# Rotated query columns of two heads in one stationary operand of 128 columns, rotation in blocks of 64 partitions

## The chip, the cores and the metric

The kernel is one program on one core of a Trainium2 chip. It is measured in microseconds (us) of device time of one launch. All arithmetic that matters is in 32-bit floats; a product of two such matrices is made from three products of operands that are split into a high part and a low part.

## What is computed

The program runs two blocks of a model over 256 tokens of width 1024. Its first mixer is a latent attention of 8 heads, and the change lies in there. Cut to what matters:

```python
def mla_mixer(x, w_dq, q_norm_g, w_uq, w_dkv, kv_norm_g, w_ukv, w_o):
    cq = rms_norm(x @ w_dq, q_norm_g)                          # 256 x 384
    q = (cq @ w_uq).reshape(b, s, H, NOPE + ROPE)              # 8 heads of 128 + 64 columns
    ckv_kr = x @ w_dkv                                         # 256 x (256 + 64)
    ckv = rms_norm(ckv_kr[..., :KV_LORA], kv_norm_g)
    kv = (ckv @ w_ukv).reshape(b, s, H, NOPE + V)
    k_nope, v = kv[..., :NOPE], kv[..., NOPE:]
    q_nope = q[..., :NOPE]
    q_rope = apply_rope(q[..., NOPE:], cos[:, None, :], sin[:, None, :])
    k_rope = apply_rope(ckv_kr[..., KV_LORA:], cos, sin)       # one for all heads
    # per head: softmax((q_nope k_nope^T + q_rope k_rope^T) * scale) @ v
    return o.reshape(b, s, H * V) @ w_o
```

Behind it come a gated feed-forward layer with a short convolution, a differential attention, two more feed-forward layers, a hybrid mixer, and a last feed-forward layer.

## The kernel before, in words

Five instruction streams are written out by hand, one for each engine (`sp`, `pe`, `act`, `dve`, `pool` in the code), and they meet at semaphores. There is no scheduler: the order of each engine is the order in which its code is written, and an engine that waits holds back all that is written behind the wait.

**Units of weights.** The weights come from HBM in units. Units 0 and 1 are `w_dq`, 2 and 3 `w_dkv`, 4 to 7 `w_uq` (`U_UQ`, two heads or 384 columns each, three chunks of 128 rows), 8 and 9 `w_ukv` (`U_UKV`), 10 to 13 `w_o`. A unit passes four stages, with two slots of each buffer, so unit u follows unit u - 2 in its slot:

- SyncE (`load_unit`, L397 to L415) loads it into `raw_u` in two DMAs, for the first and the second half of its chunks (one chunk and two for units 4 to 7). It waits until ScalarE and VectorE have split unit u - 2.
- ScalarE (`split_u`, L1302) rounds it into `hi_u`. It waits for the landing of each half and for the last use of unit u - 2 by TensorE (`used_u`).
- VectorE (`split_half`, L1787) writes the rest into `lo_u`.
- TensorE multiplies. It may start on the first chunk when that half is split, and waits for the other (`rest_ready`, L646) ahead of the second chunk.

**Queries.** For each unit of `w_uq` TensorE (L836 to L862) makes the two heads' 128 plain columns (`features_out`, 9 matmuls a head, the weights stationary, 128 columns of them) and then the two heads' 64 rotated columns (9 matmuls a head, 64 columns of stationary operand, into partitions 0 to 63 of a PSUM bank). ScalarE copies the plain part to `m_q` (L1530). VectorE (L2012 to L2027) rotates the rotated part of both heads at once: a product with the cosines over 64 partitions and 512 elements, two products with the sines over 32 partitions, which write across to the other half, and an addition into `m_qr`. `m_qr` and the rotated key `m_kr` have zeros in partitions 64 to 127. TensorE then waits for VectorE's reads of a bank before it writes that bank again (`m_qr_read`), and before it starts unit 9 it waits for all four rotations (`m_qr_out`, L874).

**Keys.** VectorE rotates the key token by token in `kr3` (L2000 to L2004), TensorE transposes it (L861), ScalarE copies it to `m_kr` (L1528). Then TensorE makes keys and values from units 8 and 9, and the attention over 8 heads follows.

The functions around this are below, with the line numbers of the profile.

## Time and profile before

| | |
|---|---|
| Three runs | 1192.35 us median, 1192.18 to 1193.42 |
| Span of the profiled execution, first to last instruction | 1190.5 us (its time outside the span is not recorded apart) |
| TensorE busy | 1150.6 us, 97% of the span |
| VectorE, ScalarE, GpSimd busy | 809.4, 702.7, 52.4 us |
| Read from HBM | 192.84 MB |
| Mean granted TensorE clock | 0.998 of full speed |

PE is TensorE, PEld its weight loads, DVE VectorE, ACT ScalarE, POOL GpSimd, SP SyncE and SPq its DMA issues. A busy time of PE counts from the start of a matmul to its modelled end, and matmuls overlap, so the cost of one is read from the distance of two starts. Every row has its start in us from the start of the span. Where the text says a "gap", the engine was idle before the row for the time in square brackets. The latent attention's queries, keys and values fill 28.2 to 58.3 us of the span.

### The profile page before, as it was taken

To read this page: it belongs to the slowest core of one execution; us is meant where nothing else is said; L and a number is where in the kernel's file an instruction comes from. 1 tells how busy PE (TensorE), PEld (TensorE's weight loads), DVE (VectorE), ACT (ScalarE), POOL (GpSimd) and SP (SyncE) were. 2 spreads that over 40 slices of the span, in tenths; PEclk is the share of its full clock that TensorE was granted. 3 is DMA by queue.
4 is the path that set the end of the run, shared out by engine and by line. 5 is a ranking of instruction groups with operands and counts; after the bars stand their busy time and mean duration, and the time that the engine had idled before them with its cause. 6 is when DMAs were issued, how large, how long until landed. Compare 5 with 4: busy or idle time off the path is not lost. (4 is left out here: it accounts for less than half of the span.)

```text
span 1190.5 us, 19157 instructions
## 1 busy us (share of the span) xinstructions
PE 1150.6 (97%) x6611; PEld 983.5 (83%) x6611; DVE 809.4 (68%) x1206; ACT 702.7 (59%) x1218; POOL 52.4 (4%) x74
## 2 busy tenths in 40 slices
PE   9999999999999989999999999999989999999997
PEld 7977888888799868888887888888977877888886
DVE  6855888888656568888877665565656756656555
ACT  6455666666566557766666554555565655555543
POOL 0200000000100010000001000000000320000000
PEclk9999999999999999999999999999999999999999
DMA  7515566667244446666673666653674016767661
GB/s 229 184 41 167 158 198 209 187 183 242 86 142 141 145 127 190 200 189 192 195 211 99 201 191 182 207 156 112 196 217 147 1 36 174 211 176 197 186 168 62
DMA packets 241057, 194.56 MB, mean 163 GB/s; under 512 B 11214, under 2 KB 223792, under 8 KB 241008
## 3 DMA queue, kind: packets, MB, share of 16 engines
q1 hardware_dynamic: 240928, 193.88, 54.1%
q8 instruction: 30, 0.49, 0.2%
q14 instruction: 19, 0.16, 0.0%
q10 hardware_dynamic: 80, 0.03, 0.0%
HBM read 192.84 MB, written 1.05 MB: 163 GB/s over the span
## 5 line engine op out<-in xcount | busy, mean ns | idle before, releaser
L767 PE MATMUL psum<-act_hl,hi_u 128*128 128x512 f32 x1312 | 327.6, 392 | 3.1 <-DVE lo_u L1813 3.1
L1813 DVE TENSOR_TENSOR lo_u<-raw_u,hi_u 128x2048 fp32r<-128x2048 f32 x103 | 236.1, 2292 | 88.4 <-ACT hi_u L1319 56.1
L767 PEld LDWEIGHTS psum<-act_hl,hi_u 128*128 128x128 f32 x1312 | 240.9, 188 | 50.5 <-issue 3.7
L770 PEld LDWEIGHTS psum<-act_hl,lo_u 128*128 128x128 f32 x1312 | 179.0, 190 | 12.8
L770 PE MATMUL psum<-act_hl,lo_u 128*128 128x256 f32 x1312 | 182.9, 282 | 0.0
L1439 ACT ACTIVATE arena<-psum 128x256 f32<-128x256 f32 x174 | 66.1, 380 | 157.0 <-PE psum L770 146.7
L1920 DVE TENSOR_TENSOR arena<-psum,arena 128x256 f32<-128x256 f32 x174 | 73.6, 423 | 106.0 <-ACT arena L1439 105.9
L622 PE MATMUL psum<-hi_d,hid_hi 128*128 128x512 f32 (+1 forms) x352 | 138.8, 394 | 1.6 <-DVE hid_lo L1937 1.6
L1337 ACT ACTIVATE hi_u<-raw_u 128x2048 fp32r<-128x2048 f32 x72 | 137.3, 1907 | 4.2 <-DMA raw_u<-in_ffn_w_gu 4.0
L623 PE MATMUL psum<-lo_d,hid_hi 128*128 128x512 f32 (+1 forms) x352 | 137.9, 392 | 0.0
L624 PE MATMUL psum<-hi_d,hid_lo 128*128 128x512 f32 (+1 forms) x352 | 137.0, 389 | 0.0
L1930 DVE SCALAR_TENSOR_TENSOR arena<-arena,vecs 128x255 f32<-128x255 f32 x176 | 85.0, 483 | 42.4 <-ACT arena L1447 31.4
L1818 DVE TENSOR_TENSOR lo_d<-raw_d,hi_d 128x1024 fp32r<-128x1024 f32 x88 | 106.6, 1216 | 3.1 <-ACT hi_d L1346 3.1
L1796 DVE TENSOR_TENSOR lo_u<-raw_u,hi_u 128x1024 fp32r<-128x1024 f32 (+4 forms) x74 | 79.4, 1108 | 43.1 <-ACT hi_u L1316 42.5
L622 PE MATMUL psum<-act_hl,hi_u 128*128 128x256 f32 (+1 forms) x320 | 92.3, 288 | 8.2 <-DVE lo_u L1796 7.6
L1346 ACT ACTIVATE hi_d<-raw_d 128x1024 fp32r<-128x1024 f32 x88 | 91.6, 1046 | 0.0
L623 PE MATMUL psum<-act_hl,hi_u 128*128 128x256 f32 (+1 forms) x320 | 90.3, 282 | 0.0
L624 PE MATMUL psum<-act_hl,lo_u 128*128 128x256 f32 (+1 forms) x320 | 90.2, 282 | 0.0
L1316 ACT ACTIVATE hi_u<-raw_u 128x1024 fp32r<-128x1024 f32 (+4 forms) x60 | 54.1, 948 | 52.4 <-PE psum L624 36.7
L1447 ACT ACTIVATE arena<-arena,vecs 128x256 f32<-128x256 f32 x88 | 52.9, 602 | 46.6 <-DVE arena L1920 45.6
L622 PEld LDWEIGHTS psum<-hi_d,hid_hi 128*128 128x128 f32 (+1 forms) x352 | 66.4, 189 | 16.1 <-issue 4.5
L624 PEld LDWEIGHTS psum<-hi_d,hid_lo 128*128 128x128 f32 (+1 forms) x352 | 66.1, 188 | 14.6
(263 smaller groups left out, 1739.7 us busy)
## 6 DMA issues: line engine op xcount, KB each, us to landing
raw_u<-in_ffn_w_up SPq DMA_DIRECT2D x88, 512.0 KB, 5.5
raw_d<-in_ffn_w_down SPq DMA_DIRECT2D x86, 512.0 KB, 3.5
raw_u<-in_ffn_w_gu SPq DMA_DIRECT2D x84, 512.0 KB, 5.6
raw_u<-in_diff_w_qkv SPq DMA_DIRECT2D x24, 512.0 KB, 4.6
raw_u<-in_w_in SPq DMA_DIRECT2D x24, 512.0 KB, 4.5
raw_u<-in_mla_w_o SPq DMA_DIRECT2D x8, 512.0 KB, 3.9
raw_u<-in_diff_w_o SPq DMA_DIRECT2D x8, 512.0 KB, 3.8
raw_u<-in_w_out SPq DMA_DIRECT2D x8, 512.0 KB, 4.3
```

The lines of the kernel that those rows point to most:

```text
L622: pe.matmul(o, s_hi, m_hi, start=start, stop=False)
L623: pe.matmul(o, s_hi, m_lo, start=False, stop=False)
L624: return pe.matmul(o, s_lo, m_hi, start=False, stop=stop)
L767: pe.matmul(o, hi[:, k, :], act_hl[:, k].rearrange("p a t -> p (a t)"), start=k == 0, stop=False)
L770: mm = pe.matmul(o[:, SEQ:], lo[:, k, :], act_hl[:, k, 0, :], start=False, stop=k == KC - 1)
L1337: act.activation(u_slot(hi_u, u0), u_slot(raw_u, u0), ACT.Copy).then_inc(S("hi_u_done"), 1)
L1346: act.activation(hi_d[:, d_slot(d) if b is None else d % 2, :], raw_d[:, d % 2, :], ACT.Copy)\
L1796: dve.tensor_tensor(v[0][:, r], v[1][:, r], v[2][:, r].bitcast(F32), ALU.subtract)\
L1813: dve.tensor_tensor(v[0], v[1], v[2].bitcast(F32), ALU.subtract).then_inc(S("lo_u_done"), 1)
L1818: dve.tensor_tensor(lo_d[:, slot, :], raw_d[:, d % 2, :], hi_d[:, slot, :].bitcast(F32), ALU.subtract).then_inc(S("lo_d_done"), 1)
L1920: dve.tensor_tensor(up_sum[:, slot, part, :], psum[:, 4 + 2 * slot + part, 0:SEQ], cross[:, slot, part, :], ALU.add).then_inc(S("up_sum"), ...
L1930: dve.scalar_tensor_tensor(buf[0:n, slot, o], up_sum[0:n, slot, part, x], vecs[0:n, bass.ds(w, 1)], buf[0:n, slot, o], ALU.mult, ALU.add). ...
```

## The change

The two heads' rotated columns of a unit become one stationary operand of 128 columns, so 9 matmuls over 128 columns stand in place of 18 over 64. For that the columns have to lie side by side in `raw_u`, in the order head 0 first half, head 1 first half, head 0 second half, head 1 second half, which puts the halves 64 partitions apart in PSUM. The loads do the sorting: each half of a unit 4 to 7 comes in six DMAs (`ROPE_BESIDE`: two of 128 columns, four of 32) in place of one. The semaphore counts follow (`half_landed`). The tables of cosines and sines grow to 128 partitions. The rotation works on 128 partitions and 256 elements, and the sine products on 64. `m_qr` holds two heads in each slot with no zeros; `m_kr` has two copies, each with zeros where the other head's rows are, and is written by four small copies after a transpose of a doubled key (`kr_twice`). In VectorE's stream the split of the next unit is now ahead of the rotation, not behind it, and the rotations have two sets of scratch buffers. TensorE's wait for a free bank (`m_qr_read`) becomes a wait for the rotation two units back (`m_qr_out`), ahead of the rotated matmuls alone.

```diff
+ROPE_BESIDE = [(0, 0, NOPE), (NOPE, NOPE + ROPE, NOPE), (256, 128, 32), (288, 320, 32), (320, 160, 32), (352, 352, 32)]
+def half_landed(u):
+    return sum(16 * len(ROPE_BESIDE) if U_UQ <= x < U_UKV else 16 for x in range(u % 2, u + 1, 2))
@@ SyncE, load_unit
-                    sp.dma_start(unit_view(raw_u, u)[:, k0:k1], units[u][:, k0:k1]).then_inc(S(landed), 16)
+                    dst, src = unit_view(raw_u, u)[:, k0:k1], units[u][:, k0:k1]
+                    if U_UQ <= u < U_UKV:
+                        for at, c0, n in ROPE_BESIDE:
+                            sp.dma_start(dst[:, :, at:at + n], src[:, :, c0:c0 + n]).then_inc(S(landed), 16)
+                        continue
+                    sp.dma_start(dst, src).then_inc(S(landed), 16)
@@ TensorE, mla
-                        pe.wait_ge(S("m_qr_read"), i - 1)
                     for h in range(2):
-                        mm = features_out(psum[:, b, h * SEQ:h * SEQ + SEQ], u, h * 192, NOPE)
+                        mm = features_out(psum[:, b, h * SEQ:h * SEQ + SEQ], u, h * NOPE, NOPE)
                     mm.then_inc(S("m_q_up"), 1)
-                    for h in range(2):
-                        mm = features_out(psum[0:ROPE, b + 1, h * SEQ:h * SEQ + SEQ], u, h * 192 + NOPE, ROPE)
+                    if i >= 2:
+                        pe.wait_ge(S("m_qr_out"), i - 1)
+                    mm = features_out(psum[:, 5 + 2 * (i % 2), 0:SEQ], u, 2 * NOPE, 2 * ROPE)
                     mm.then_inc(S("used_u"), 1)
@@ TensorE, scores
-                        mm = pe.matmul(o, m_qr[:, h, tok(t)], m_kr, start=False, stop=True)
+                        mm = pe.matmul(o, m_qr[:, h // 2, tok(t)], m_kr[:, h % 2, :], start=False, stop=True)
@@ ScalarE, mla
-                        act.activation(m_kr[0:ROPE], psum[0:ROPE, 3, 0:SEQ], ACT.Copy).then_inc(S("m_kr_out"), 1)
+                        act.wait_ge(S("m_rope_zeros"), 1)
+                        for e in range(2):
+                            for r in (slice(32 * e, 32 * e + 32), slice(64 + 32 * e, 96 + 32 * e)):
+                                act.activation(m_kr[r, e, :], psum[r, 3, 0:SEQ], ACT.Copy).then_inc(S("m_kr_out"), 1)
@@ VectorE, mla
-                dve.tensor_tensor(kr3[:, 2], kr3[:, 0], kr3[:, 1], ALU.add).then_inc(S("k_roped"), 1)
+                for t in range(TT):
+                    a, b = (kr3[:, i, t, :].rearrange("p (c n) -> p c n", c=2).unsqueeze(2).broadcast_to([P, 2, 2, 32])
+                            for i in range(2))
+                    dve.tensor_tensor(kr_twice[:, t], a, b, ALU.add).then_inc(S("k_roped"), 1)
...
+                    if i >= 2:
+                        dve.wait_ge(S("m_qr_out"), i - 1)
                     dve.wait_ge(S("used_u"), U_UQ + i + 1)
-                    raw = psum[0:ROPE, 4 + 2 * (i % 2) + 1, :].rearrange("p (h t) -> p h t", h=2)
-                    ch.put(dve.tensor_tensor(t1, raw, both(ropeq[:, 0, :]), ALU.mult))
-                    ch.put(dve.tensor_tensor(t2[0:32], raw[32:64], both(ropeq[32:64, 1, :]), ALU.mult))
-                    dve.tensor_tensor(t2[32:64], raw[0:32], both(ropeq[0:32, 1, :]), ALU.mult)\
-                        .then_inc(S("m_qr_read"), 1)
+                    split_u(U_UQ + i + 2)
+                    raw = psum[:, 5 + 2 * (i % 2), 0:SEQ]
+                    ch.put(dve.tensor_tensor(t1, raw, ropeq[:, 0, :], ALU.mult))
+                    for c in range(2):
+                        src, dst = slice(64 * c, 64 * c + 64), slice(64 - 64 * c, 128 - 64 * c)
+                        ch.put(dve.tensor_tensor(t2[dst], raw[src], ropeq[src, 1, :], ALU.mult))
                     ch.wait()
-                    dve.wait_ge(S("m_qr_read"), i + 1)
-                    dve.tensor_tensor(m_qr[0:ROPE, 2 * i:2 * i + 2, :], t1, t2, ALU.add).then_inc(S("m_qr_out"), 1)
-                    split_u(U_UQ + i + 2)
+                    dve.tensor_tensor(m_qr[:, i, :], t1, t2, ALU.add).then_inc(S("m_qr_out"), 1)
@@ VectorE, start
-            dve.memset(m_qr[ROPE:], 0.0).then_inc(S("m_rope_zeros"), 1)
-            dve.memset(m_kr[ROPE:], 0.0).then_inc(S("m_rope_zeros"), 1)
+            dve.memset(m_kr, 0.0).then_inc(S("m_rope_zeros"), 1)
```

SyncE's stream at the loads of units 6, 7 and 8, before the change (`w_uq` is units 4 to 7, `w_ukv` 8 and 9; one DMA a row):

```order
L414 DMA raw_u<-in_mla_w_uq 128x384 [waits lo_u_done,hi_u_done]
L414 DMA raw_u<-in_mla_w_uq 128x2x384
L414 DMA raw_u<-in_mla_w_uq 128x384 [waits lo_u_done,hi_u_done]
L414 DMA raw_u<-in_mla_w_uq 128x2x384
L414 DMA raw_u<-in_mla_w_ukv 128x1024 [waits lo_u_done,hi_u_done]
L414 DMA raw_u<-in_mla_w_ukv 128x1024
```

The same place now, units 7 and 8 ("x4" stands for four DMAs; L426 is the new loop):

```order
L426 DMA raw_u<-in_mla_w_uq 128x128 [waits lo_u_done,hi_u_done]
L426 DMA raw_u<-in_mla_w_uq 128x128
L426 DMA raw_u<-in_mla_w_uq 128x32 x4
L426 DMA raw_u<-in_mla_w_uq 128x2x128 x2
L426 DMA raw_u<-in_mla_w_uq 128x2x32 x4
L428 DMA raw_u<-in_mla_w_ukv 128x1024 [waits lo_u_done,hi_u_done]
L428 DMA raw_u<-in_mla_w_ukv 128x1024
```

A unit of `w_uq` now takes 12 DMA issues in place of 2, 48 in place of 8 for the four, and the loads of units 8 and 9 stand behind them in the same stream.

VectorE's stream from the rotation of unit 6 to the values of unit 8, before (`lo_u` rows are splits of units 8 and 9, `masks` is the scratch buffer of the rotation):

```order
L1991 SCALAR_TENSOR_TENSOR act_hl<-psum,vecs,act_hl 128x256 [waits latent_hi] x2
L2020 TENSOR_TENSOR masks<-psum,arena 64x512 [waits m_qr_out,used_u]
L2021 TENSOR_TENSOR masks<-psum,arena 32x512
L2022 TENSOR_TENSOR masks<-psum,arena 32x512
L2026 TENSOR_TENSOR arena<-masks 64x512 [waits m_qr_read,dve_chain_mla]
L1796 TENSOR_TENSOR lo_u<-raw_u,hi_u 128x1024 [waits hi_u_half]
L1796 TENSOR_TENSOR lo_u<-raw_u,hi_u 128x1024 [waits hi_u_done]
L2020 TENSOR_TENSOR masks<-psum,arena 64x512 [waits m_qr_out,used_u]
```

And now:

```order
L2009 SCALAR_TENSOR_TENSOR act_hl<-psum,vecs,act_hl 128x256 [waits latent_hi] x2
L1814 TENSOR_TENSOR lo_u<-raw_u,hi_u 128x1024 [waits hi_u_half,used_u,m_qr_out]
L1814 TENSOR_TENSOR lo_u<-raw_u,hi_u 128x1024 [waits hi_u_done]
L2041 TENSOR_TENSOR masks<-psum,arena 128x256
L2044 TENSOR_TENSOR masks<-psum,arena 64x256 x2
L2046 TENSOR_TENSOR arena<-masks 128x256 [waits dve_chain_mla]
L1814 TENSOR_TENSOR lo_u<-raw_u,hi_u 128x1024 [waits hi_u_half,used_u,m_qr_out]
```

The split of the unit that is to be loaded and rounded next now stands ahead of the rotation of the unit that TensorE has just finished; a rotation that was behind only its own matmuls is now behind a split as well.

## Rows read from the trace of the kernel before

**Rows 1.** The page: busy times and TensorE's granted clock.

```profile
PE 1150.6 (97%) x6611; PEld 983.5 (83%) x6611; DVE 809.4 (68%) x1206; ACT 702.7 (59%) x1218; POOL 52.4 (4%) x74
PEclk9999999999999999999999999999999999999999
```

**Rows 2.** Stretches: length, busy us and instructions of each engine, clock, DMA share, GB/s.

```profile
40.00:52.00 12.00, 11.36 (x87) 10.59 (x86) 11.67 (x16) 6.09 (x7) 0.00 (x0) 1.00 0.58 213
```

**Rows 3.** PE's timeline: start, us, line, out<-in, shapes [gap <- who ended it].

```profile
28.22 0.28 PE L622 MATMUL psum<-act_hl,hi_u 128*128 128x256 f32 x1
...
30.37 0.28 PE L622 MATMUL psum<-act_hl,hi_u 128*64 128x256 f32 x1
...
32.42 0.28 PE L622 MATMUL psum<-act_hl,hi_u 128*128 128x256 f32 x1
...
45.80 0.28 PE L624 MATMUL psum<-act_hl,lo_u 128*64 128x256 f32 x1
...
47.31 0.36 PE L622 MATMUL psum<-act_hl,hi_u 128*128 128x256 f32 x1 [0.43 <-DVE lo_u L1796]
...
52.63 0.28 PE L622 MATMUL psum<-act_hl,hi_u 128*128 128x256 f32 x1
```

**Rows 4.** DVE's timeline, 30 to 54 us, and one row of the attention.

```profile
31.29 1.51 DVE L1796 TENSOR_TENSOR lo_u<-raw_u,hi_u 128x384 fp32r<-128x384 f32 x2
32.72 0.67 DVE L2020 TENSOR_TENSOR masks<-psum,arena 64x512 f32<-64x512 f32 x1
...
35.53 1.41 DVE L1796 TENSOR_TENSOR lo_u<-raw_u,hi_u 128x384 fp32r<-128x384 f32 x2
...
41.22 0.86 DVE L1991 SCALAR_TENSOR_TENSOR act_hl<-psum,vecs,act_hl 128x256 fp32r<-128x256 f32 x2
...
49.90 2.35 DVE L1796 TENSOR_TENSOR lo_u<-raw_u,hi_u 128x1024 fp32r<-128x1024 f32 x2
...
68.81 0.42 DVE L2051 TENSOR_TENSOR act_hl<-psum,act_hl 128x256 fp32r<-128x256 f32 x1 [1.14 <-ACT act_hl L1561]
```

**Rows 5.** SPq's timeline, DMA issues: start, us, out<-in.

```profile
1.65 0.42 SPq L468 DMA_DIRECT2D ident<-in_ident  x1
...
9.04 0.36 SPq L486 DMA_DIRECT2D arena<-in_ropek  x1
...
18.15 0.34 SPq L414 DMA_DIRECT2D raw_u<-in_mla_w_uq  x1
18.53 1.15 SPq L414 DMA_DIRECT2D raw_u<-in_mla_w_uq  x1
...
32.88 0.82 SPq L414 DMA_DIRECT2D raw_u<-in_mla_w_uq  x2
...
285.46 0.50 SPq L494 DMA_DIRECT2D dist<-in_dist  x1
...
287.96 0.91 SPq L499 DMA_DIRECT2D crows<-in_crows  x1
...
290.64 0.43 SPq L464 DMA_DIRECT2D gain_row<-in_norm_g  x1
```

**Rows 6.** DMA issues of one unit of `w_uq`: count, KB, us from issue to landing.

```profile
raw_u<-in_mla_w_uq SPq DMA_DIRECT2D x1, 384.0 KB, 3.3
raw_u<-in_mla_w_uq SPq DMA_DIRECT2D x1, 192.0 KB, 2.4
```

**Rows 7.** DMA queue 1 from 284.8 to 291.1 us: packets, MB, share of 16 engines.

```profile
q1 hardware_dynamic: 1504, 2.04, 96.9%
```

**Rows 8.** ACT's timeline.

```profile
24.03 0.83 ACT L1316 ACTIVATE hi_u<-raw_u 128x768 fp32r<-128x768 f32 x1
...
38.22 0.82 ACT L1510 ACTIVATE act_hl<-psum,vecs 128x256 fp32r<-128x256 f32 x2
38.94 0.37 ACT L1528 ACTIVATE arena<-psum 64x256 f32<-64x256 f32 x1
```

**Rows 9.** PE's waits over the program: for whom, us in total, times, longest.

```profile
PE psum L1017 <- DVE normed L2102: 2.7, 1, 2.7
```

More of the change, by code:

```diff
@@ L121, in constants @@
         "ropek": np.concatenate([tok(cos2), tok(sin2)], 1).reshape(P, -1),
-        "ropeq": np.concatenate([cos2.T, sin2.T], 1), "masks": masks.reshape(P, -1),
+        "ropeq": np.concatenate([np.tile(cos.T, (4, 1)), np.concatenate([sin.T, sin.T, -sin.T, -sin.T], 0)], 1), "masks": masks.reshape(P, -1),
     }
@@ L332, in program @@
         m_q = ar(0, H, SEQ)
-        m_qr = ar(2048, H, SEQ)
+        m_qr = ar(2048, 4, SEQ)
+        m_kr = ar(3072, 2, SEQ)
         m_k = ar(4096, H, SEQ)
         m_v = ar(6144, TT, H, VD)
-        m_kr = ar(8192, SEQ)
         ropek = ar(8448, 2, TT, ROPE)
-        ropeq = ar(8704, 2, SEQ, p=ROPE)
+        ropeq = ar(8704, 2, SEQ)
         m_p = ar(9216, 3, TT, SEQ)
@@ L343, in program @@
         kr3 = normed[:].rearrange("p a b -> p (a b)")[:, 1280:1664].rearrange("p (a t n) -> p a t n", a=3, t=TT)
-        qr2 = masks[0:ROPE, :, :].rearrange("p (a b) t -> p a (b t)", a=2).rearrange("p a (b t) -> p a b t", b=2)
+        kr_twice = normed[:].rearrange("p a b -> p (a b)")[:, 1664:1920].rearrange("p (t c e n) -> p t c e n", t=TT, c=2, e=2)
+        qr2 = masks[:].rearrange("p (i a b) t -> p i a (b t)", i=2, a=2)
         d_q = ar(0, H, SEQ)
@@ L842, in mla @@
                         pe.wait_ge(S("latents"), 4)
-                        pe.wait_ge(S("k_roped"), 1)
+                        pe.wait_ge(S("k_roped"), 2)
                     if i >= 2:
                         pe.wait_ge(S("m_q_out"), i - 1)
-                        pe.wait_ge(S("m_qr_read"), i - 1)
                     for h in range(2):
-                        mm = features_out(psum[:, b, h * SEQ:h * SEQ + SEQ], u, h * 192, NOPE)
+                        mm = features_out(psum[:, b, h * SEQ:h * SEQ + SEQ], u, h * NOPE, NOPE)
                     mm.then_inc(S("m_q_up"), 1)
-                    for h in range(2):
-                        mm = features_out(psum[0:ROPE, b + 1, h * SEQ:h * SEQ + SEQ], u, h * 192 + NOPE, ROPE)
+                    if i >= 2:
+                        pe.wait_ge(S("m_qr_out"), i - 1)
+                    mm = features_out(psum[:, 5 + 2 * (i % 2), 0:SEQ], u, 2 * NOPE, 2 * ROPE)
                     mm.then_inc(S("used_u"), 1)
@@ L860, in mla @@
                         for t in range(TT):
-                            mm = pe.transpose(psum[0:ROPE, 3, t * P:t * P + P], kr3[:, 2, t, :], ident[:])
+                            mm = pe.transpose(psum[:, 3, t * P:t * P + P], kr_twice[:, t].rearrange("p c e n -> p (c e n)"), ident[:])
                         mm.then_inc(S("latent_tr"), 1)
@@ L869, in mla @@
                     if i == 0:
-                        pe.wait_ge(S("m_kr_out"), 1)
+                        pe.wait_ge(S("m_kr_out"), 4)
                     else:
@@ L914, in values @@
                     mm.then_inc(S("m_values"), 1)
-                pe.wait_ge(S("m_rope_zeros"), 2)
+                pe.wait_ge(S("m_rope_zeros"), 1)
                 pe.wait_ge(S("m_k_out"), 1)
@@ L1314, in split_u @@
                             if u in BY_HALVES:
-                                act.wait_ge(S(f"raw_half{i}_{u % 2}"), 16 * (u // 2 + 1))
+                                act.wait_ge(S(f"raw_half{i}_{u % 2}"), half_landed(u))
                             act.activation(unit_view(hi_u, u)[:, part], unit_view(raw_u, u)[:, part], ACT.Copy)\
@@ L1325, in split_part @@
                 if u in BY_HALVES:
-                    act.wait_ge(S(f"raw_half{part}_{u % 2}"), 16 * (u // 2 + 1))
+                    act.wait_ge(S(f"raw_half{part}_{u % 2}"), half_landed(u))
                 elif part == 0:
@@ L2009, in mla @@
                 split_u(5)
-                t1, t2 = qr2[:, 0], qr2[:, 1]
-                both = lambda v: v.unsqueeze(1).broadcast_to([v.shape[0], 2, SEQ])
                 for i in range(4):
@@ L2014, in mla @@
                         latent_lo(range(3, 5))
+                    t1, t2 = qr2[:, i % 2, 0], qr2[:, i % 2, 1]
+                    if i >= 2:
+                        dve.wait_ge(S("m_qr_out"), i - 1)
                     dve.wait_ge(S("used_u"), U_UQ + i + 1)
-                    if i:
-                        dve.wait_ge(S("m_qr_out"), i)
-                    raw = psum[0:ROPE, 4 + 2 * (i % 2) + 1, :].rearrange("p (h t) -> p h t", h=2)
-                    ch.put(dve.tensor_tensor(t1, raw, both(ropeq[:, 0, :]), ALU.mult))
-                    ch.put(dve.tensor_tensor(t2[0:32], raw[32:64], both(ropeq[32:64, 1, :]), ALU.mult))
-                    dve.tensor_tensor(t2[32:64], raw[0:32], both(ropeq[0:32, 1, :]), ALU.mult)\
-                        .then_inc(S("m_qr_read"), 1)
+                    split_u(U_UQ + i + 2)
[4 more added lines that the diff above has]
+                        ch.put(dve.tensor_tensor(t2[dst], raw[src], ropeq[src, 1, :], ALU.mult))
                     ch.wait()
-                    dve.wait_ge(S("m_qr_read"), i + 1)
-                    dve.tensor_tensor(m_qr[0:ROPE, 2 * i:2 * i + 2, :], t1, t2, ALU.add).then_inc(S("m_qr_out"), 1)
-                    split_u(U_UQ + i + 2)
+                    dve.tensor_tensor(m_qr[:, i, :], t1, t2, ALU.add).then_inc(S("m_qr_out"), 1)
                 for i in range(2):
```

## The prediction

> **What bounds the kernel now.** I read the page first: TensorE is busy for 97% of the span at full clock in all 40 slices [rows 1], so what shortens its stream shortens the kernel, unless another engine or a load is as late. Then the stretches around the change: from 40 to 52 us TensorE is busy for 11.36 us of 12, but VectorE for 11.67 [rows 2]. Two engines are full there, and both have to become shorter. Then the timelines. TensorE goes through unit 4 from 28.22 to 32.42 without a gap and ends unit 7 at about 45.92 (the last start, 45.80, and one pitch). Its only small gaps follow, for the split of unit 8, whose second chunk starts at 47.31; unit 9 starts at 52.63 [rows 3]. Behind unit 9 the attention is a chain over the same engines that the change leaves alone, so all that counts is when unit 9 starts. A shift there is a shift of the end.
>
> **TensorE's saving.** In unit 4, 18 matmuls on 128 columns take 30.37 - 28.22 = 2.15 us, 0.1195 each, and 18 on 64 columns take 32.42 - 30.37 = 2.05, 0.114 each [rows 3]: half the columns, nearly the same time. Nine on 128 columns cost 1.07. That saves 0.98 us a unit, 3.9 for four. The transposes of the doubled key and the scores' matmuls keep their count and their moving columns, so they cost nothing new (at most the difference of 0.005 a matmul).
>
> **VectorE's saving.** A rotation runs from 32.72 to 35.53, 2.81 us for four operations of 512 elements [rows 4]. Now they have 256, for which a row shows 0.42 with PSUM as a source [rows 4], against 0.67 before. Four by about 0.45 with their chain wait is 1.8 us, so 1.0 less a rotation. Bounds: 0.42 is the least that a row shows, 0.70 (no gain) the most. The doubled key costs one more addition, under 0.42, before the split of unit 5. That split's second part ended at about 32.8 before [rows 4], and now at about 33.1.
>
> **If the loads were in time** those two would give the gain. Unit 5 can't go past its first chunk before 33.2, so it ends at 36.1, the transposes at 36.7; units 6 and 7 take 3.2 each, so unit 7 ends at 43.2 against 45.92, and unit 9 starts near 49.5 against 52.63: 3 us faster.
>
> **The loads.** They are what I think is late next. A unit is now 12 issues on SyncE in place of 2. The first issue after a wait takes 0.34 and a pair 0.82 [rows 5], so one that follows another takes 0.43 or so, and with the 0.04 between issues its pitch is 0.475. Other rows bound it: `ropek`, 128 rows of one run each, 0.36, a pitch of 0.40; `ident`, 128 runs of 512 bytes, 0.42; and in the nearest thing to the new stream, a long row of issues back to back, six issues from 285.46 start 0.50 apart until 287.96 [rows 5]. Size hardly matters, the count does. I take 0.475, bounds 0.40 and 0.50. Now and then an issue is much longer: 1.15 at 18.53 and 0.91 at 287.96 [rows 5]. I keep the one at 18.53 (0.72 over) and no second; two would be the bound.
>
> The issues of unit 4 start at 18.15, as before. With no waiting in between, 12 issues a unit, SyncE is through with unit 4 at 18.15 + 5.7 + 0.72 = 24.6, unit 5 at 30.3, unit 6 at 36.0, unit 7 at 41.7; before, unit 7 was issued by 33.7 [rows 5]. The split two units back, for which a load waits, is earlier each time. From issue to landing one DMA of 192 KB takes 2.4 us, one of 384 KB 3.3 [rows 6]; for 32 KB I take 2.1, between 1.6 (twice 2.4, less 3.3) and 2.4. The second part of unit 7 then lands at 41.2 + 2.1 = 43.3. The DMA engines themselves are not the limit: 1504 packets of 1356 bytes in the mean took 96.9% of 16 engines for 6.3 us, 65 ns each [rows 7]; at that price a unit's 2304 packets on 16 engines would be 9.4 us, but at 256 bytes in the mean they are a fifth of the size; if the price went by bytes alone (590 KB of 2.04 MB in 6.1 us) it would be 1.8 us. I take under 5.7 us, the time of the issues; above it is part of the slow bound.
>
> The Trainium skill, "DMA: Bandwidth & Descriptors", section "Issuing engines are not separate DMA queues", holds the sequencer's time to start a DMA to be usually small beside the DMA itself. By that rule the loads would stay hidden, and the sum would be the gain of 3 us. The rows speak against it here: 0.43 of issue [rows 5] for a DMA that moves 16 KB, where 192 KB land in 2.4 [rows 6].
>
> **The path through the late loads.** The second part of a unit takes ScalarE 0.83 [rows 8] and VectorE about 0.95 more (1.41 for both parts, less the first) [rows 4], 1.85 with the hand-over. Unit 7, landed at 43.3, is split at 45.15. TensorE has by then finished unit 6 (landed at 37.6, split at 39.45, so that it ends at 42.5) and waits; 24 matmuls from 45.3 on take 2.9, to 48.2. That is 2.3 later than before.
>
> Then the new order on VectorE adds its part, since each rotation stands behind a split. From 45.15: rotation of unit 5 1.8, the two low latents 0.8, split of unit 8 2.25, rotation of unit 6 1.8, split of unit 9 2.25 (2.35 for two overlapping [rows 4]), rotation of unit 7 1.8: together 10.7, at 55.85. ScalarE is no later: it goes from 44.15 through two latents, 0.75, four key copies at 0.27 (0.37 for one alone), a query copy 0.5 and the first half of unit 8 by 47.5, before VectorE needs it at 47.75 [rows 8]. The waits that the change adds cost nothing here: `m_qr_out` of two units back is long there. TensorE ends unit 8 at 50.15 + (52.63 - 47.31) = 55.5 [rows 3], and waits for the last rotation before unit 9: 56.0 against 52.63, **3.4 us later**.
>
> Other edits: VectorE's clearing at the start falls from two memsets to one, while it waits for the first root; nothing. The larger `ropeq` table is loaded long before its first use; nothing. Query copies, stores and all later units are as before, nothing.
>
> **Sum.** On the profiled execution 1190.5 + 3.4 = 1193.9 of span. The median of the runs is 1.85 above that span, and I carry this over: 1192.35 + 3.4 = 1195.75.
>
> **The rivals.**
>
> *The loads stay hidden, and it is faster.* Small DMAs would have to issue in about 0.2 us. For it: TensorE was the bound before, and both savings are plain in the rows. Against: no row of 128 partitions issues in under 0.33. Sum: 3.0 less, 1189.4. 8%.
>
> *A draw.* With a pitch of 0.40, as for `ropek`, and no long issue, unit 7's second part lands at 39.6, its split ends at 41.5, TensorE ends unit 7 at 44.5, 1.4 earlier than before, and the chain on VectorE from 41.5 ends at 52.2 against the 52.63 at which unit 9 started. So the saving is spent and nothing is lost: 1192.3. At 0.44 it is 1.2 later. 24%.
>
> *Slower by more.* A pitch of 0.50 and two long issues put unit 7's landing 1.9 later and the end at 5.4 more: 1197.7. A DMA price that does matter would give the same. 13%.
>
> *The clock falls.* In my walk TensorE stands still for 1.8 and 2.4 us, before the second chunks of units 6 and 7, close to one another. In the profile it stood still for 2.7 us [rows 9] and the clock stayed at full speed in every slice [rows 1]. If it fell to 1.2 GHz, the matmuls of units 7 and 8 (2.9 and 5.3 us) would take twice as long for a part, 4 us more on top: 1199.8. 5%. The Trainium skill, "TensorE: Matmul & The Clock Gate", section "HAM oscillation — how this bites in real kernels", names waits for a transfer between short bursts of matmuls as what loses the clock; no slice of this trace shows a loss.
>
> **How the numbers follow.** The forecast of 1195.75 holds 50%, with its own range from 1194.3 to 1197.3 (pitch 0.45 to 0.49). A measurement of this kernel can tell 0.2%, 2.4 us. Faster by more needs the hidden loads, 0.08. Within 2.4 us lies the draw and the lower end of the forecast, pitches up to 0.45 or 0.46: 0.28. Slower: 0.64. The range for 8 in 10 goes from 1191.6 (a pitch under 0.40 with little else) to 1198.4.
>
> **What would show it.** In the changed profile: SyncE's issues of `in_mla_w_uq` as an unbroken row of 48 from 18.15 to about 41.7, at 0.475 apart; ScalarE waiting for `raw_u` by DMA ahead of the second part of units 4, 6 and 7, where now it waits for TensorE; TensorE gaps ended by `lo_u` before units 6 and 7's second chunks, and one ended by the rotation before unit 9, which starts at 56.0. Rotations of 1.8 us. The forecast is wrong if SyncE is done by 38 (a draw or better), if unit 9's start is moved but the end is not, or if the clock row falls below 9.

## The result, and the profile after

| | median (range) of the runs | ratio to the kernel before, 95% interval |
|---|---|---|
| kernel before, the same chip | 1192.69 us (1192.18 to 1193.42), 4 runs | |
| changed kernel | 1198.51 us (1197.66 to 1200.62), 4 runs | 1.0051 [1.0039, 1.0064] |

The change makes the kernel 5.8 us slower. I had said 3.4 us slower, 1195.75, with 1198.4 as the upper end. The direction and the cause came as forecast, the size did not. The median lies 0.1 us above that end; the profiled execution, 1197.66, lies 0.7 under it.

The page of the changed kernel, for [rows 1]:

```profile
span 1195.8 us, 19105 instructions
PE 1149.0 (96%) x6561; PEld 982.4 (82%) x6575; DVE 804.5 (67%) x1206; ACT 703.4 (59%) x1221; POOL 50.3 (4%) x74
PEclk9899999999999999999999999999999999999999
```

No engine has more to do than before, but for 0.7 us of ScalarE, and the span is 5.3 us longer. So the time is waiting, and the clock row has one slice below 9, the second. SyncE's timeline of its DMA issues (start, us, count) shows where the waiting begins:

```profile
19.23 25.47 SPq L426 DMA_DIRECT2D raw_u<-in_mla_w_uq  x48
44.80 4.16 SPq L428 DMA_DIRECT2D raw_u<-in_mla_w_ukv  x4
```

Forty-eight issues stand in one unbroken row of 25.47 us. Before, the eight were done by 33.70 [rows 5], now the 48 are done at 44.70. Single issues of that row, from narrow stretches of the same timeline, are one with a single run a partition (20.08), two with two runs a partition (23.91 and 44.22), two that took much longer, and the pair at 40.21 and 41.07, between which SyncE stood still for 0.43 us (40.21 is the last issue of unit 7's first part):

```profile
20.08 0.43 SPq L426 DMA_DIRECT2D raw_u<-in_mla_w_uq  x1
...
20.56 1.37 SPq L426 DMA_DIRECT2D raw_u<-in_mla_w_uq  x1
...
23.91 0.47 SPq L426 DMA_DIRECT2D raw_u<-in_mla_w_uq  x1
...
40.21 0.43 SPq L426 DMA_DIRECT2D raw_u<-in_mla_w_uq  x1
...
41.07 0.38 SPq L426 DMA_DIRECT2D raw_u<-in_mla_w_uq  x1
...
43.03 1.15 SPq L426 DMA_DIRECT2D raw_u<-in_mla_w_uq  x1
...
44.22 0.47 SPq L426 DMA_DIRECT2D raw_u<-in_mla_w_uq  x1
```

The last issue of unit 7 starts at 44.22. ScalarE's waits name the landing (engine, tile, line, who ended it: us in total, times, longest):

```profile
ACT hi_u L1331 <- DMA raw_u<-in_mla_w_uq: 16.3, 7, 3.5
```

In its timeline the second part of unit 7 starts at 46.24, right on the landing:

```profile
46.24 0.84 ACT L1331 ACTIVATE hi_u<-raw_u 128x768 fp32r<-128x768 f32 x1 [3.49 <-DMA raw_u<-in_mla_w_uq]
```

VectorE's timeline from there on is the chain that I had laid out, with no gap of weight in it. The counterparts of [rows 4] are a rotation, the low latents, a split of 1024 columns, and so on to the last rotation:

```profile
47.12 0.96 DVE L1814 TENSOR_TENSOR lo_u<-raw_u,hi_u 128x768 fp32r<-128x768 f32 x1 [3.71 <-ACT hi_u L1331]
48.11 0.42 DVE L2041 TENSOR_TENSOR masks<-psum,arena 128x256 f32<-128x256 f32 x1
48.56 0.87 DVE L2044 TENSOR_TENSOR masks<-psum,arena 64x256 f32<-64x256 f32 x2
49.47 0.42 DVE L2046 TENSOR_TENSOR arena<-masks 128x256 f32<-128x256 f32 x1
49.93 0.88 DVE L2009 SCALAR_TENSOR_TENSOR act_hl<-psum,vecs,act_hl 128x256 fp32r<-128x256 f32 x2
50.95 2.36 DVE L1814 TENSOR_TENSOR lo_u<-raw_u,hi_u 128x1024 fp32r<-128x1024 f32 x2
...
54.94 2.35 DVE L1814 TENSOR_TENSOR lo_u<-raw_u,hi_u 128x1024 fp32r<-128x1024 f32 x2
...
58.69 0.42 DVE L2046 TENSOR_TENSOR arena<-masks 128x256 f32<-128x256 f32 x1
```

And TensorE, for [rows 3]: a gap before unit 4, gaps before the second chunks of units 6, 7 and 8, and unit 9 only behind the last rotation:

```profile
30.61 0.39 PE L636 MATMUL psum<-act_hl,hi_u 128*128 128x256 f32 x1 [2.14 <-DVE act_hl L2009]
...
41.26 0.36 PE L636 MATMUL psum<-act_hl,hi_u 128*128 128x256 f32 x1 [1.40 <-DVE lo_u L1814]
...
48.22 0.37 PE L636 MATMUL psum<-act_hl,hi_u 128*128 128x256 f32 x1 [3.49 <-DVE lo_u L1814]
...
53.46 0.36 PE L636 MATMUL psum<-act_hl,hi_u 128*128 128x256 f32 x1 [0.27 <-DVE lo_u L1814]
...
59.26 0.36 PE L636 MATMUL psum<-act_hl,hi_u 128*128 128x256 f32 x1 [0.30 <-DVE arena L2046]
```

The gap before unit 4 was in no part of the forecast: in VectorE's stream the low part of the query latents (29.29) stands behind the split of unit 4's second part (28.20), which waited for its load. Unit 7 is later still, so this gap is not what moves the end.

Unit 9 starts at 59.26 instead of 52.63 [rows 3], 6.6 us later. To see whether that shift stays, one instruction behind the attention is a good marker: a split on ScalarE that stands in every version. In the kernel before and in the changed one:

```profile
82.31 1.99 ACT L1316 ACTIVATE hi_u<-raw_u 128x1024 fp32r<-128x1024 f32 x2
```

```profile
88.98 1.99 ACT L1331 ACTIVATE hi_u<-raw_u 128x1024 fp32r<-128x1024 f32 x2
```

It is 6.7 later. The two profiled executions keep that distance until about 860 us. There TensorE waits for splits of weights that ScalarE could not start before they landed, and one such gap became shorter. Two of TensorE's rows before and the same two now:

```profile
855.91 0.35 PE L622 MATMUL psum<-act_hl,hi_u 128*128 128x256 f32 x1 [1.23 <-DVE lo_u L1796]
...
866.20 0.35 PE L622 MATMUL psum<-act_hl,hi_u 128*128 128x256 f32 x1 [2.44 <-DVE lo_u L1796]
```

```profile
862.62 0.36 PE L636 MATMUL psum<-act_hl,hi_u 128*128 128x256 f32 x1 [1.22 <-DVE lo_u L1814]
...
871.88 0.35 PE L636 MATMUL psum<-act_hl,hi_u 128*128 128x256 f32 x1 [1.43 <-DVE lo_u L1814]
```

The distance is 6.71 at the first and 5.68 at the second, and the ends are 5.3 apart. In e4_sort_in_split below, 2.2 us ahead at the marker, the same stretch goes the other way: 2.5 ahead at the first of these matmuls, 3.7 at the second. So a shift at unit 9 is not the shift of the end to the microsecond. Below, "marker" is this split's start less 82.31.

### The profile page after: what moved, and what is told of

Its sections match the earlier page's. It is cut to its first block and busy times, and to the rows that moved or that the text cites. A ratio compares the mean times of both kernels' runs of the same rounds, so it can differ in the third digit from the quotient of the medians.

```text
span 1195.8 us, 19105 instructions
## 1 busy us (share of the span) xinstructions
PE 1149.0 (96%) x6561; PEld 982.4 (82%) x6575; DVE 804.5 (67%) x1206; ACT 703.4 (59%) x1221; POOL 50.3 (4%) x74
## 5 line engine op out<-in xcount | busy, mean ns | idle before, releaser
L784 PE MATMUL psum<-act_hl,lo_u 128*128 128x256 f32 x1312 | 182.9, 282 | 0.0
L636 PE MATMUL psum<-act_hl,hi_u 128*128 128x256 f32 x308 | 90.8, 295 | 13.3 <-DVE lo_u L1814 10.2
L637 PE MATMUL psum<-act_hl,hi_u 128*128 128x256 f32 x308 | 88.5, 287 | 0.0
L638 PE MATMUL psum<-act_hl,lo_u 128*128 128x256 f32 x308 | 88.5, 287 | 0.0
```

The costliest lines, as they stand in the source:

```text
L636: pe.matmul(o, s_hi, m_hi, start=start, stop=False)
L637: pe.matmul(o, s_hi, m_lo, start=False, stop=False)
L638: return pe.matmul(o, s_lo, m_hi, start=False, stop=stop)
L784: mm = pe.matmul(o[:, SEQ:], lo[:, k, :], act_hl[:, k, 0, :], start=False, stop=k == KC - 1)
```

## The experiments

The theory: the changed kernel is slower because a unit needs 12 issues on SyncE; without them the change is a gain. The rivals: the larger table or the new order on VectorE costs the time, the transfers are slow because their runs are short, or the half clock costs it. Ratios are to the kernel before on the same chip. It took 1192.69 us beside the changed kernel, 1193.49 beside e1, e2, e3 and e6, 1192.45 beside e5, e10, e11 and e12, and 1193.91 beside e13, e4 and e7, so rows of different groups are compared by their ratios.

| experiment | median, us | ratio, 95% interval | SyncE done with unit 7 | marker |
|---|---|---|---|---|
| changed kernel | 1198.51 | 1.0051 [1.0039, 1.0064] | 44.7 | +6.7 |
| e1_plain_loads | 1189.63 | 0.9968 [0.9956, 0.9980] | 33.8 | -2.3 |
| e2_loads_only | 1199.80 | 1.0052 [1.0038, 1.0065] | 44.7 | +6.7 |
| e3_rope_first | 1197.43 | 1.0034 [1.0021, 1.0047] | 44.0 | +5.3 |
| e6_table | 1193.59 | 1.0002 [0.9992, 1.0011] | 33.9 | +0.2 |
| e5_filled | 1199.28 | 1.0058 [1.0043, 1.0072] | 43.8 | +5.6 |
| e12_long_runs | 1207.20 | 1.0122 [1.0107, 1.0137] | 51.3 | +13.6 |
| e13_tiny_extra | 1198.87 | 1.0042 [1.0029, 1.0056] | 43.7 | +7.3 |
| e10_three_loads | 1194.19 | 1.0014 [1.0005, 1.0023] | 35.9 | +1.4 |
| e11_three_rope_first | 1192.61 | 0.9997 [0.9988, 1.0006] | 35.8 | -0.4 |
| e4_sort_in_split | 1190.38 | 0.9973 [0.9962, 0.9984] | 34.0 | -2.2 |
| e7_sort_rope_first | 1190.83 | 0.9977 [0.9967, 0.9987] | 34.3 | -2.1 |

**e1_plain_loads**, the change without its loads. The columns stay unsorted, so each head's queries are made from other columns than the reference's.

```diff
-                    if U_UQ <= u < U_UKV:
-                        for at, c0, n in ROPE_BESIDE:
-                            sp.dma_start(dst[:, :, at:at + n], src[:, :, c0:c0 + n]).then_inc(S(landed), 16)
-                        continue
                     sp.dma_start(dst, src).then_inc(S(landed), 16)
```

> The changed kernel with each half of a unit of w_uq loaded by one DMA as before, so that the query columns are multiplied unsorted (the rotated part of the scores is another). Theory A (the 12 issues a unit on SyncE make the loads late, and that is all of the loss): the gain of the fewer matmuls appears, unit 9 starts near 49.5 to 50 us, about 2.5 to 3 us before its start in the kernel before, and the kernel takes about 1190, 0.2 to 0.25% less than before. Theory B (the rotation behind the split, or the stationary operand of 128 columns, carries the loss): it stays 3 us or more above the kernel before, near 1196. Theory C (the falls of the clock carry it): the clock stays full here, since the waits are gone, so C can't be told from A by the time, only by the filled kernel.

It is 3.8 us faster than the kernel before. With the issues gone, the rest of the change is a gain, and the forecast's 3 us for it was about right. The first matmul of unit 9 on TensorE:

```profile
50.28 0.36 PE L631 MATMUL psum<-act_hl,hi_u 128*128 128x256 f32 x1 [0.39 <-DVE arena L2041]
```

That is 2.35 us before the 52.63 of [rows 3]. I had written 49.5 from TensorE's stream alone; VectorE's chain sets it here too, 0.8 later. TensorE's own saving is there: unit 6 takes it from 36.60 to 39.90, 3.31 us, where it took from 37.43 to 41.71 before, 4.27. That is 0.97 less, and I had 0.98.

**e2_loads_only**, the kernel before with 12 issues a unit and nothing else.

```diff
+SIX = [(0, 128), (192, 128), (128, 32), (160, 32), (320, 32), (352, 32)]
...
+                    if U_UQ <= u < U_UKV:
+                        for at, n in SIX:
+                            sp.dma_start(dst[:, :, at:at + n], src[:, :, at:at + n]).then_inc(S(landed), 16)
+                        continue
```

> The kernel before, computing the same, with only the loads of w_uq cut: six DMAs for each half of a unit, to the places where the columns lay. Theory A: all of the loss and more, since the matmuls are the old ones: unit 7's second part lands near 46, unit 9 starts near 59.5 in place of 52.63, 6 to 7 us slower, near 1199. Theory B: under 1 us slower.

6.2 us slower: the loads alone cost all that the change costs, and what the change saves elsewhere does not show under them. Its SyncE issues, and ScalarE's second part of unit 7:

```profile
19.05 25.61 SPq L424 DMA_DIRECT2D raw_u<-in_mla_w_uq  x48
```

```profile
46.12 0.84 ACT L1328 ACTIVATE hi_u<-raw_u 128x768 fp32r<-128x768 f32 x1 [2.71 <-DMA raw_u<-in_mla_w_uq]
```

Both starts are within 0.2 us of the changed kernel's. Unit 9 starts at 59.29, where I had 59.5 and the changed kernel has 59.26. What stands last before it is another thing: here the last rotation is over at 56.6 and TensorE goes from unit 8 to unit 9 without a gap, there the last rotation holds it.

**e3_rope_first**, the changed kernel with each rotation ahead of the split.

```diff
-                    split_u(U_UQ + i + 2)
                     raw = psum[:, 5 + 2 * (i % 2), 0:SEQ]
...
                     dve.tensor_tensor(m_qr[:, i, :], t1, t2, ALU.add).then_inc(S("m_qr_out"), 1)
+                    split_u(U_UQ + i + 2)
```

> The changed kernel with VectorE's rotation ahead of the split of the next unit, as it was. Theory A: the landing of unit 7 (near 46.2) stays, behind it the last rotation is no longer behind the split of unit 9, and TensorE goes from unit 8 to unit 9 without a wait: 0.5 to 0.8 us less than the changed kernel, near 1198. Theory B (the order is the cause): 3 us less or more, at most 1195.5.

It gets 1.1 us by medians and 2.0 by ratios, whose intervals overlap, and 1.4 at the marker. Of this 1.4 the row of issues explains 0.7, for it ended that much earlier (44.0 against 44.7). So the order on VectorE is a small part, near the 0.5 to 0.8 that I expected, and the late load the large one.

**e6_table**, the kernel before with the rotation's table on 128 partitions, half of it unused.

```diff
-        "ropeq": np.concatenate([cos2.T, sin2.T], 1)
+        "ropeq": np.tile(np.concatenate([cos2.T, sin2.T], 1), (2, 1))
```

> The kernel before with the table of cosines and sines loaded for 128 partitions (256 KB in place of 128), used as before. The profile of the changed kernel has the load of unit 2 landing 1 us later and so the first load of w_uq issued 1.07 us later (19.22 against 18.15). Theory A: the larger table does that, in a stretch where the DMA engines are full; the first issue for w_uq moves by 0.4 to 1 us, and the kernel before has slack for it: its time stays within 0.5 us. Rival: the 1 us is chance of one run, and the issue stays at 18.1 to 18.3.

No difference. This matters for one number: SyncE begins with unit 4 at 19.23 in the changed kernel and at 18.15 before [rows 5], and I suspected the table. But the start is 18.54 here and 19.05 in e2_loads_only, which has the old table, and 18.14 and 18.34 in e5_filled and e3_rope_first, which have the new one. Over all 13 profiled executions it lies between 18.14 and 19.23, with the old table and with the new one.

**e5_filled**, the changed kernel with matmuls of zeros while TensorE would stand idle.

```diff
+            def fill(n, bank):
+                for _ in range(n):
+                    pe.matmul(psum[:, bank, 0:SEQ], zeros[:, 0:P], zeros[:, 0:SEQ], start=True, stop=True)
...
+                fill(18, 2)
                 pe.wait_ge(S("latent_lo"), 3)
...
+                                          filled=(0, 0, 12, 30)[i] if h == 0 else 0)
```

> The changed kernel with matmuls of zeros put where TensorE idled for 2.14 us (18 before the latents' low parts) and while it waits for the second part of units 6 and 7 (12 and 30), into banks that are written afresh afterwards; they keep the granted clock at full speed through the stage. Theory (the two stretches at 0.51 and 0.52 of the clock are hidden, the first behind unit 6's late load, the second behind VectorE's splits): clock 1.00 throughout the stage, and the time within 0.7 us of the changed kernel's 1198.5, that is 1197.8 to 1199.2. Rival (the slow stretches are on the path: each costs 1.7 us of TensorE's work): 1195.0 to 1197.0.

The reason for it is in the stretches of the changed kernel (length, busy us of PE, PEld, DVE, ACT, POOL, granted clock, DMA share, GB/s):

```profile
28.00:31.30 3.30, 1.16 (x9) 0.90 (x8) 2.93 (x9) 2.60 (x9) 1.00 (x3) 1.00 0.46 107
31.30:34.70 3.40, 3.40 (x19) 3.40 (x18) 2.08 (x6) 1.26 (x2) 3.08 (x7) 0.51 0.42 80
34.70:38.00 3.30, 3.30 (x29) 3.30 (x29) 1.04 (x2) 0.71 (x2) 1.37 (x2) 0.99 0.51 113
...
44.00:48.30 4.30, 0.81 (x8) 0.63 (x6) 1.15 (x2) 2.03 (x5) 0.00 (x0) 1.00 0.70 182
48.30:51.70 3.40, 3.40 (x17) 3.40 (x18) 3.12 (x7) 3.33 (x7) 0.00 (x0) 0.52 0.92 325
```

Twice TensorE runs at half speed (1.2 of 2.4 GHz), behind gaps of 2.14 and 3.49 us. With the filler both stretches are at full speed:

```profile
31.30:34.70 3.40, 3.15 (x27) 2.97 (x26) 1.63 (x3) 1.33 (x2) 3.08 (x6) 1.00 0.35 68
...
48.30:51.70 3.40, 2.60 (x22) 2.43 (x21) 3.18 (x6) 3.35 (x5) 0.00 (x0) 1.00 0.92 348
```

and the time is the same, 1199.28. Its unit 9 starts at 58.17, 1.1 before the changed kernel's 59.26, but its row of issues also began 1.1 earlier. So the half clock cost nothing that these rows show: the first time unit 6 was late anyway (its second chunk starts at 40.94 with the filler and at 41.26 without), the second time VectorE's chain was.

**e12_long_runs**, the kernel before with 12 issues a unit whose runs are all 512 bytes long.

```diff
+                        for p0 in (0, 64):
+                            for at in (0, 128, 256):
+                                sp.dma_start(dst[p0:p0 + 64, :, at:at + 128], src[p0:p0 + 64, :, at:at + 128])\
+                                    .then_inc(S(landed), 16)
```

> The kernel before, computing what it computes, with each part of units 4 to 7 loaded by 6 transfers (12 a unit) as the loads-only version had, but cut into 2 halves of 64 partitions by 3 column ranges of 128, so that every run is 512 bytes long. Theory (the count of issues): 48 issues at 0.475 us, some 0.9 us less than with two runs a partition; SyncE's last issue at about 43.5 to 44; 1198.0 to 1199.5, within 1 us of the loads-only version's 1199.8. Rival (runs under 512 bytes): as the kernel before, 1192.5 to 1194.5.

Both theories missed: 14.75 us slower than before. The rival is refuted, since long runs did not help; the theory had the right place and a wrong price, for an issue to 64 partitions took longer than one to 128:

```profile
18.58 32.74 SPq L422 DMA_DIRECT2D raw_u<-in_mla_w_uq  x48
...
22.65 0.60 SPq L422 DMA_DIRECT2D raw_u<-in_mla_w_uq  x1
```

The row of issues ends 6.7 later than in e2_loads_only and the marker is 6.9 later. The experiment changed two things at once, so it was no clean test of the runs' length; the next one is.

**e13_tiny_extra**, the kernel before with its own whole loads and five transfers of 8 bytes a partition ahead of each.

```diff
+                    if U_UQ <= u < U_UKV:
+                        for n in range(5):
+                            at = 10 * (u - U_UQ) + 5 * part + n
+                            sp.dma_start(spare[:, 2 * at:2 * at + 2], units[u][:, k0, 2 * at:2 * at + 2]).then_inc(S("spare_in"), 16)
                     sp.dma_start(unit_view(raw_u, u)[:, k0:k1], units[u][:, k0:k1]).then_inc(S(landed), 16)
```

> The kernel before, computing what it computes, with its own two whole loads for each of units 4 to 7, but five tiny transfers (8 bytes into each of 128 partitions, to a spare place that nobody reads or waits for) issued ahead of each of the two parts: 12 issues a unit as in the changed kernel, the bytes and the run lengths of the kernel before. Theory (SyncE's issues): the last issue of unit 7 stands at 43.5 to 45 us and the time is that of the loads-only version, 1198.0 to 1200.0 (unit 7's own part is one transfer of 256 KB that needs some 0.8 us more to land than small ones, TensorE's stretches otherwise alike). Rival (the short runs of the sorted loads slow the transfers): the plain loads land in time and the time stays at the kernel before's, 1192 to 1194.5.

Forty transfers that move 40 KB together cost 5.0 us by medians (7.3 at the marker). A tiny one issues as slowly as the sorted columns did, and what a unit needs comes last:

```profile
34.17 0.43 SPq L418 DMA_DIRECT2D spare<-in_mla_w_uq  x1
...
43.24 0.44 SPq L419 DMA_DIRECT2D raw_u<-in_mla_w_uq  x1
```

Here the data are moved in the same two transfers as before, and they are not slower: the last one, issued at 43.24, lands 3.5 us later, and before it took 3.4. The number of issues is enough to explain the loss; short runs aren't needed for it.

**e10_three_loads** and **e11_three_rope_first**: another order of the sorted columns needs three transfers a part, and the swap of halves then goes by 32 partitions. The second also rotates ahead of the split.

```diff
-ROPE_BESIDE = [(0, 0, NOPE), (NOPE, NOPE + ROPE, NOPE), (256, 128, 32), (288, 320, 32), (320, 160, 32), (352, 352, 32)]
+ROPE_BESIDE = [(0, 0, 160), (160, 320, 64), (224, 160, 160)]
...
-                    for c in range(2):
-                        src, dst = slice(64 * c, 64 * c + 64), slice(64 - 64 * c, 128 - 64 * c)
+                    for c in range(4):
+                        src, dst = slice(32 * c, 32 * c + 32), slice(96 - 32 * c, 128 - 32 * c)
```

> The changed kernel with another order of the sorted columns (first head's plain and first rotary half; then the rest of the second head's first half and its second half side by side; then the first head's second half with the second head's plain columns), which needs 3 transfers a part instead of 6; the swap in the rotation then goes by 32 partitions in 4 operations of 32x256 instead of 2 of 64x256. Everything the reference asks for is computed. Theory (SyncE's issue time): 6 issues a unit at 0.48 us are 2.9 us a unit, less than TensorE's 4.2, so the loads go back behind TensorE and no wait on the unit's load is left after unit 5; unit 9 starts at about 50.3 (as with plain loads) plus up to 1.7 us for the two more rotation operations of 0.43 us in each of the last two units: 51.2 to 52.0. Time 1189.7 to 1191.5 against the kernel before's 1193.5, ratio about 0.9975. Rival (short runs slow the transfers themselves, whatever the issue): runs of 256 bytes are left in one of three transfers and the wait stays: 1195 to 1197.

> As the three-transfer version, and VectorE rotates unit 4+i before it splits unit 6+i. Theory: rotation first took 1.1 us off the changed kernel because it feeds TensorE's reuse of the bank earlier; here VectorE's chain sets unit 9 as with plain loads, so it is worth 0 to 1 us: 1189.0 to 1190.8. Rival: splits come 2.6 us later than TensorE wants them at units 6 and 7, since the loads are in time now: 1 to 2 us slower than without the reordering, 1191 to 1193.

SyncE was done at 35.9, but the load is not in time, though I had expected it to be. ScalarE waits for unit 7's second part:

```profile
38.45 0.84 ACT L1331 ACTIVATE hi_u<-raw_u 128x768 fp32r<-128x768 f32 x1 [1.65 <-DMA raw_u<-in_mla_w_uq]
```

Unit 7's first issue stands at 33.06, as with plain loads (33.00), but six issues in a row take 2.8 us where two take 0.8, and its second part lands at 38.43 in place of 36.77. VectorE adds the rest, in the first of the two kernels:

```profile
39.33 0.96 DVE L1814 TENSOR_TENSOR lo_u<-raw_u,hi_u 128x768 fp32r<-128x768 f32 x1 [1.84 <-ACT hi_u L1331]
40.32 0.42 DVE L2041 TENSOR_TENSOR masks<-psum,arena 128x256 f32<-128x256 f32 x1
40.77 1.77 DVE L2044 TENSOR_TENSOR masks<-psum,arena 32x256 f32<-32x256 f32 x4
```

The products with the sines take 1.77 in four operations where two took 0.88, and three rotations (units 5, 6 and 7) stand in the chain and not the two that I had counted. Unit 9 starts at 53.92, 3.6 later than with plain loads: 1.7 of it is the later split of unit 7 (39.33 against 37.67), which is the load, and 2.0 the longer chain behind it.

The time of the first, 1194.19, lies between the theory's range and the rival's, and its ratio is just above 1. The second, 1192.61, lies where its rival had it, but not for the rival's reason, since rotation first still gained 1.6 us here.

**e4_sort_in_split** and **e7_sort_rope_first**: whole loads, and the columns are sorted where ScalarE and VectorE write the split parts anyway.

```diff
+def sorted_parts(dst, src, k0, k1):
+    h2 = lambda v: v.rearrange("p k (h n) -> p k h n", h=2)
+    out = [(h2(dst[:, k0:k1, 0:2 * NOPE]), h2(src[:, k0:k1])[:, :, :, 0:NOPE])]
+    for k in range(k0, k1):
+        out.append((dst[:, k, 2 * NOPE:].rearrange("p (c h n) -> p c h n", c=2, h=2),
+                    src[:, k, :].rearrange("p (h r) -> p h r", h=2)[:, :, NOPE:].rearrange("p h (c n) -> p c h n", c=2)))
+    return out
```

> The changed kernel with the two whole loads a unit of the kernel before; the columns are sorted where ScalarE and VectorE split a unit into its two halves, by one operation of 256 columns a row block and one of 128 for each of the 3 row blocks. Everything is computed. Theory: loads go back behind TensorE as in the plain-loads version (1189.6); VectorE pays some 0.1 us more for a first and 0.15 to 0.3 us for a second part, and the chain that sets unit 9 holds units 5 (second part), 6 and 7: 0.6 to 1.2 us later than with plain loads. 1190.0 to 1191.2, ratio to the kernel before 0.9975 to 0.9985. Rival (small strided operations cost 0.4 us and more each, so the chain grows by 2.5 us): 1192 to 1193.5, no gain.

> The version that sorts in the split, with VectorE rotating unit 4+i before it splits unit 6+i. Theory: in the three-transfer pair rotation first was worth 1.6 us of the median, because the rotation of unit 7's predecessor is what TensorE waits for at unit 9; here the chain is 2 us shorter and the same order is worth 0.5 to 1.5 us: 1189.0 to 1190.3. Rival: with the chain shorter the split is the later of the two things that TensorE wants, and rotation first costs 0 to 1 us: 1190.5 to 1192.

Everything is computed, and e4 is 3.2 us faster than the kernel before (0.9973 [0.9962, 0.9984] of 1193.9), about 9 faster than the changed one. Its price on VectorE for unit 7, in two parts, and the start of unit 9 on TensorE:

```profile
37.16 0.63 DVE L1827 TENSOR_TENSOR lo_u<-raw_u,hi_u 128x256 fp32r<-128x256 f32 x2 [0.57 <-ACT hi_u L1337]
38.01 1.09 DVE L1827 TENSOR_TENSOR lo_u<-raw_u,hi_u 128x512 fp32r<-128x512 f32 x3 [0.23 <-ACT hi_u L1337]
```

```profile
50.38 0.36 PE L640 MATMUL psum<-act_hl,hi_u 128*128 128x256 f32 x1 [0.30 <-DVE arena L2062]
```

With plain loads the two parts took 0.56 and 0.96, so the sorting costs 0.2 us a unit on VectorE, and unit 9 starts 0.1 later than there. Rotation first adds nothing to it: 1190.83 lies inside e4's range, and in the rival's. My 0.5 to 1.5 us did not come, and TensorE shows what the rival named. The split is now what it waits for, ahead of unit 8, and behind that it reaches unit 9 at 50.54 without a gap:

```profile
44.18 0.36 PE L640 MATMUL psum<-act_hl,hi_u 128*128 128x256 f32 x1 [0.39 <-DVE lo_u L1830]
```

In e4 unit 8 starts at 43.52.

## Why the prediction was wrong in size

**Right: what it removes.** A rotation is 1.8 us (48.11 to 49.93), as said, and TensorE's 0.97 us a unit in e1_plain_loads is my 0.98. The change without its loads gains 3.8 us by medians and 2.3 at the marker, and I had 3.

**Right: what is late next, and the path behind it.** The 48 issues as an unbroken row, ScalarE waiting on the landing, the split, VectorE's chain and the last rotation ahead of unit 9 all came in this order. The chain took from 48.08 (the end of unit 7's split) to 59.11, 11.0 us, where I had 10.7. The landing comes 2.0 us after its issue, and I had 2.1.

**Wrong: the loads' term.** "SyncE is through with ... unit 7 at 41.7", so that its second part "lands at 43.3". It was through at 44.7 and the part landed at 46.2, 2.9 of the 3.3 us by which unit 9 missed my 56.0. The parts of the term, from the single issues of the changed kernel:

- The pitch. 0.475 was right for issues with one run a partition. Those of a second part have two; all but the first of them take 0.47, with a pitch of 0.51, and the first issue of the next unit comes 0.1 late: together 0.8 us over 48 issues, so 0.49 in the mean. I had read "size hardly matters, the count does" from rows that did not have two runs one behind the other.
- The long issues. I kept one of 0.72 over. There were two, 0.9 and 0.7 over, and the pause of 0.43 before 41.07, which is no issue. Together 1.3 us more. This is the rule and not bad luck: each of the six rows of 48 issues in these runs has two long issues, one among its first six and one between 36.3 and 43.0 us, and a pause of 0.43 or 0.44 ahead of its 43rd issue.
- The start at 19.23 instead of 18.15, 1.1 us. That is chance of the profiled execution, and says nothing of the median: with a start at 18.14 e5_filled has its unit 9 at 58.17, still 2.2 over my 56.0.

Less 0.1 for the first issue of the row, which takes only 0.34, these are the 3.0 us between 41.7 and 44.7.

**Wrong the other way: "A shift there is a shift of the end."** The 6.6 us at unit 9 were 5.3 at the end of the profiled execution, as the rows at 866 us show. The loads' term was 3.0 us too small and the carrying over 1.3 us too large, so it is partly luck that the median came within 2.8 us of my 1195.75.

Of the rivals, "slower by more" (13%) is what happened, by the second long issue, the pause that nobody had, and a mean pitch of 0.49, near its 0.50; its 1197.7 was still 0.8 short. "The clock falls" (5%) happened as well, but the 4 us that I put on it did not: the stretches at 0.51 and 0.52 stand beside something later. My ground for the 5%, a gap of 2.7 us that left the clock whole [rows 9], was weaker than I took it for. The same gap of 2.7 us, ahead of the same transposes (at 420 to 436 us), stands in all 13 traces, and in eight of them the clock fell to half beside it. Here are the stretches behind it in the kernel before and in e1_plain_loads (columns as under e5_filled, the granted clock third from the end):

```profile
422.00:426.00 4.00, 3.85 (x19) 3.26 (x20) 0.85 (x2) 1.02 (x2) 0.00 (x0) 1.00 1.11 327
```

```profile
420.00:423.30 3.30, 3.30 (x11) 2.72 (x11) 0.75 (x1) 0.69 (x1) 0.00 (x0) 0.50 1.17 325
```

"A draw" had a slip in its sum: with a pitch of 0.40 from 18.15 on and no long issue, the 48th issue starts at 36.95 and lands at 39.05, not 39.6. Together with "the loads stay hidden" it fell with the result, and e2_loads_only and e13_tiny_extra show why: no issue was cheap enough. The Trainium skill, "DMA: Bandwidth & Descriptors", section "Issuing engines are not separate DMA queues", has the time to start a DMA as usually small beside the DMA. For a single one that is so here too, 0.43 us of issue against 1.6 us or more to the landing. But the issues stand one behind the other while the transfers overlap, and so a row of 48 set the end.

What stays open: what a long issue and the pause ahead of the 43rd issue are, why SyncE's start wanders, and what exactly shifts the waits near 866 us. Medians and markers differ by up to 2.3 us in single experiments. One reason is seen: e6_table is 0.2 us behind the kernel before at the marker and at 422 us, and 1.7 at 867.90, and in between lies its fall of the clock beside the gap of 2.7. So terms under 1 us are read from the traces and not from the times.

## What to carry to other kernels

A DMA that sorts columns isn't free because the bytes are the same: count the issues, multiply by the measured pitch of the same shape, add the long ones, and lay the row beside the engine that waits. Here 2 issues a unit stayed hidden; with 6 unit 7's second part landed 1.7 us later and with 12 it landed 9.4 later. If the data pass through an engine on their way anyway, let that operation do the sorting: it cost VectorE 0.2 us a unit, where the issues cost the kernel some 6 us. And where two engines are full side by side, an edit that frees one must be checked for what it puts on the other.

## What the runs showed of the hardware

- An issue on SyncE, back to back, took 0.43 us with one run a partition whether that is 8, 128 or 512 bytes, 0.44 with two runs behind one with one run, 0.47 with two runs behind another with two, and 0.60 to 64 partitions with 512-byte runs. The first after a wait took 0.34.
- In all 13 traces one of the first six issues of `w_uq` took 1.0 to 1.6 us. The six rows of 48 had one more such issue each, and a pause of 0.43 or 0.44 us ahead of the 43rd, at 40.2 in the earliest and at 47.4 in the latest. The cause is open.
- The granted clock fell to half behind TensorE gaps of 2.14 and 3.49 us in the changed kernel, yet a gap of 2.7 [rows 9] left it whole, as did one of 2.10 in e10_three_loads (its 55 to 59.2 us are at 1.00). Beside the gap of 2.7 us that all 13 traces have, it stayed whole in five and fell in eight. The length of one gap doesn't decide by itself.
- Reading sorted columns by strides within a split cost VectorE 0.07 and 0.13 us for the two parts of a unit, in three operations more; four operations on 32 partitions took 1.77 us, two on 64 took 0.88.
